# Another order of the blocks inside the steps of a two-direction recurrence

## The reference

```python
def step(S, inp):
    r_t, w_t, kk_t, b_t, v_t, k_t = inp
    sa = jnp.einsum("bhvk,bhk->bhv", S, kk_t)
    S = (S * w_t[:, :, None, :] - sa[..., None] * b_t[:, :, None, :]
         + v_t[..., None] * k_t[:, :, None, :])
    return S, jnp.einsum("bhvk,bhk->bhv", S, r_t)
...
mod = jax.nn.silu(c) @ ada_w[l] + ada_b[l]
sh1, sc1, g1, sh2, sc2, g2 = [m[:, None, :] for m in jnp.split(mod, 6, axis=-1)]
```

## Time and profile before

| | |
|---|---|
| median of 3 runs | 1587.11 us (1568.42 to 1589.66) |
| the profiled execution | 1576.66 us, its span 1575.1 us |
| TensorE busy | 1493.3 us, 95% of the span |
| VectorE, ACT, GpSimd busy | 918.2, 598.1, 271.8 us |
| mean granted TensorE clock | 0.96 of full speed |
| the recurrence's matmuls (L898) | from 243.6 to 528.3 us of the span |

### The profile page before, as it was taken

The page is one execution under the profiler, slowest core; times in us unless marked ns, Lnnn a source line. Parts: engine busy times, 40 slices in busy tenths (PEclk is TensorE's granted clock), DMA queues, the critical chain, the costliest instruction groups (busy, mean ns, idle before and its releaser), DMA issues.

```text
span 1575.1 us, 35522 instructions
## 1 busy us (share of the span) xinstructions
PE 1493.3 (95%) x14858; PEld 1232.4 (78%) x14858; DVE 918.2 (58%) x1499; ACT 598.1 (38%) x1037; POOL 271.8 (17%) x290
## 2 busy tenths in 40 slices
PE   5999989999999998999999998998999999999997
PEld 3788865788889777887877886877878888888885
DVE  4424245676668738888886224767565655555232
ACT  4422345333343534443443223536664322232221
POOL 0000024554443010111111121000021111111110
PEclk9999999778689999999999998999999999999998
DMA  9232201222220222232323222221112232232221
GB/s 370 97 110 79 81 0 56 76 91 84 83 63 4 83 81 80 80 107 80 107 82 108 92 92 81 88 81 55 54 54 82 106 107 85 101 107 92 92 92 72
DMA packets 38987, 139.15 MB, mean 88 GB/s; under 512 B 3152, under 2 KB 3664, under 8 KB 38480
## 3 DMA queue, kind: packets, MB, share of 16 engines
q1 hardware_dynamic: 38720, 135.24, 25.2%
q10 hardware_dynamic: 144, 2.10, 0.3%
HBM read 135.22 MB, written 2.10 MB: 87 GB/s over the span
## 4 chain that ended last, share of the span: by engine, by line
PE 80%; DVE 13%; ACT 3%; issue 3%; DMA 1%; ACTq 0%; DVEq 0%; SPq 0%
PE bank L716 56%; PE bank L898 9%; DVE ffn_sb L3153 5%; PE bank L725 3%; PE bank L662 2%; PE bank L992 1%; DVE w_up L2581 1%; PE bank L1064 1%; PE bank L1004 1%; PE bank L1554 1%; PE bank L929 1%; DMA arena<-w 1%; PE bank L655 1%; ACT w_up L1675 1%; ACT arena L2171 1%
## 5 line engine op out<-in xcount | busy, mean ns | idle before, releaser
L716 PE MATMUL bank<-hf_hi,w_up 128*128 128x512 f32 x1376 | 424.2, 389 | 0.0
L716 PEld LDWEIGHTS bank<-hf_hi,w_up 128*128 128x128 f32 x1376 | 258.4, 188 | 53.2
L716 PE MATMUL bank<-hf_lo,w_up 128*128 128x512 f32 x688 | 269.2, 391 | 4.5 <-DVE w_up L2581 4.5
L716 PE MATMUL bank<-act_hi,w_down 128*128 128x512 f32 x704 | 216.9, 389 | 0.0
L898 PEld LDWEIGHTS bank<-arena 64*64 64x64 f32 x4224 | 160.7, 154 | 35.7 <-issue 25.2
L898 PE MATMUL bank<-arena 64*64 64x32 f32 (+1 forms) x4224 | 172.3, 237 | 10.1 <-issue 6.1
L1675 ACT ACTIVATE w_up<-ring 128x1024 fp32r<-128x1024 f32 x87 | 91.9, 1058 | 215.7 <-PE bank L716 215.7
L2581 DVE TENSOR_TENSOR w_up<-ring,w_up 128x1024 fp32r<-128x1024 f32 x87 | 106.9, 1229 | 96.9 <-ACT w_up L1675 96.9
L716 PEld LDWEIGHTS bank<-hf_lo,w_up 128*128 128x128 f32 x688 | 129.2, 188 | 35.9 <-DVE w_up L2581 8.9
L3153 DVE SCALAR_TENSOR_TENSOR ffn_sb<-ffn_sb 128x512 f32<-128x512 f32 x176 | 151.5, 861 | 5.4
L716 PEld LDWEIGHTS bank<-act_hi,w_down 128*128 128x128 f32 x704 | 132.2, 188 | 27.4
(11 more groups left out here) (350 smaller groups left out, 2399.7 us busy)
## 6 DMA issues: line engine op xcount, KB each, us to landing
ring<-w SPq DMA_DIRECT2D x76, 1024.0 KB, 4.9
ring<-w SPq DMA_DIRECT2D x32, 704.0 KB, 4.0
ring<-w SPq DMA_DIRECT2D x64, 256.0 KB, 3.7
arena<-w SPq DMA_DIRECT2D x8, 1024.0 KB, 18.7
x<-xT SPq DMA_DIRECT2D x1, 2048.0 KB, 9.9
x<-xT ACTq DMA_DIRECT2D x1, 2048.0 KB, 8.4
outT<-x SPq DMA_DIRECT2D x4, 512.0 KB, 2.7
arena<-ctxT SPq DMA_DIRECT2D x1, 1024.0 KB, 18.9
```

The source lines that it names most:

```text
L716: ins = mm(out, w[:, a, k, :], of_block(b, k0 + k), start=first and k == 0 and m == 0, stop=last and k == n - 1 and m == 2)
```

## The change

No instruction that computes is added or removed. The written-out lists are put in another order in all three kinds of steps and on all three engines:

- `scores(q, 1)` moves from level 3 up to right behind level 2's `nx`, ahead of `updates`, and `scores(q, 0)` behind level 2's `dx` (token steps). In the context steps they move to levels 5 and 6.
- `turned(m, 0)` and `turned(m, 1)` move from levels 3 and 4 to level 5, `ada_part(n, 0)` and `(n, 1)` from level 4 and 5 to ahead of and into level 6, `results(n, 1)` ahead of level 4's `dx`.
- `ada_select(n)`, until now in level 6, moves in the token steps to level 3 of the next step, and so does `mod_out`. Two wait counts are changed to fit: `scores(q, 1)` of a token step no longer waits for the sums of the step just before it.
- On VectorE `scores_out`, `first_level`, `running_sums` and `second_result` follow; on ACT `tok_out`, `first_result`, `state_padded`, `update_in` and `ada_row_out`.

The diff, cut to the waits and the token steps (the lists for n = -1 and for the context steps are changed in the same manner):

```diff
@@ -984,7 +984,8 @@
                 done("tok", d, before)
                 done("y_out", d, q - 2 - NCC)
                 if q > 0:
-                    pe.wait_ge(s[("ada_row", "mod")[d]], 8 + min(before, 8))
+                    rows = before - d if q > NCC else before
+                    pe.wait_ge(s[("ada_row", "mod")[d]], 8 + min(rows, 8))
                 n, keys = 2 * L if isx else L, keys_at(d, q)
                 for j in range(NJ):
                     at = slice(2 * L * j, 2 * L * j + n)
@@ -1144,7 +1145,7 @@
                 if n >= 7:
                     return
                 pe.wait_ge(s["ada_row"], 8 + n + 2)
-                done("nk", 1, 2 * n + 4 if n < NCC - 2 else 2 * n + 6)
+                done("nk", 1, 2 * n + 4 if n < NCC - 2 else 2 * n + 8)
                 done("y_out", 1, n - NCC + 1)
                 for m in range(4):
...
             for n in range(NCC - 2, NC - 1):
                 m, q = n + 1, n + 2
                 nx(m, 0, 2)
+                nx(m, 1, 2)
+                scores(q, 1)
                 updates(n, 0)
-                nx(m, 1, 2)
+                dx(m, 1, 2)
+                dx(m, 0, 2)
                 scores(q, 0)
-                dx(m, 0, 2)
-                dx(m, 1, 2)
+                updates(n, 1)
+                nx(m, 1, 3)
+                nx(m, 0, 3)
                 state_terms(n, 0)
                 if n == NC - 2:
                     gate_products(0, 1)
-                updates(n, 1)
-                nx(m, 1, 3)
-                nx(m, 0, 3)
-                scores(q, 1)
-                dx(m, 1, 3)
-                turned(m, 0)
-                dx(m, 0, 3)
                 state_terms(n, 1)
                 if n == NC - 2:
                     gate_products(1, 2)
+                if n > NCC - 2:
+                    ada_select(n - 1)
+                dx(m, 1, 3)
+                dx(m, 0, 3)
                 results(n, 0)
                 nx(m, 0, 4)
-                turned(m, 1)
                 nx(m, 1, 4)
+                results(n, 1)
                 dx(m, 0, 4)
-                results(n, 1)
-                ada_part(n, 0)
                 dx(m, 1, 4)
                 nx(m, 0, 5)
-                ada_part(n, 1)
+                turned(m, 0)
                 nx(m, 1, 5)
                 dx(m, 0, 5)
+                turned(m, 1)
                 dx(m, 1, 5)
+                ada_part(n, 0)
                 nx(m, 0, 6)
-                ada_select(n)
                 nx(m, 1, 6)
+                ada_part(n, 1)
                 dx(m, 0, 6)
                 dx(m, 1, 6)
...
@@ -2008,15 +2010,15 @@
                     for j in range(4):
                         act_f(ycv[0][:, j, :], y_conv[:, j, :], ACT.Copy).then_inc(s["h_hi"], 1)
                 decay_exps(q + 1)
+                update_in(m, 1)
+                first_result(n, 0)
+                first_result(n, 1)
+                tok_out(m, 0)
+                state_padded(m, 0)
                 tok_out(m, 1)
-                first_result(n, 0)
-                update_in(m, 1)
+                state_padded(m, 1)
                 update_in(m, 0)
-                tok_out(m, 0)
                 ada_row_out(n)
-                state_padded(m, 1)
-                first_result(n, 1)
-                state_padded(m, 0)
             split_first("W_OUT")
             for d in range(2):
                 update_out(NC - 1, d)
...
             for n in range(NCC - 2, NC - 1):
                 m, q = n + 1, n + 2
-                w_out(m, 0, 2)
-                running_sums(q + 1, 1)
                 running_sums(q + 1, 0)
                 w_out(m, 1, 2)
-                scores_out(q, 0)
+                w_out(m, 0, 2)
+                scores_out(q, 1)
                 x_out(m, 1, 2)
                 x_out(m, 0, 2)
                 x_turned(m, 0, 2)
+                scores_out(q, 0)
                 x_turned(m, 1, 2)
                 w_out(m, 1, 3)
                 w_out(m, 0, 3)
                 state_out(n, 0)
-                scores_out(q, 1)
+                if n > NCC - 2:
+                    mod_out(n - 1)
+                state_out(n, 1)
                 x_out(m, 0, 3)
                 x_out(m, 1, 3)
-                state_out(n, 1)
+                running_sums(q + 1, 1)
                 x_turned(m, 0, 3)
                 if n == NC - 2:
                     conv_low(0)
                 w_out(m, 0, 4)
-                first_level(q, 1)
+                w_out(m, 1, 4)
+                second_result(n, 0)
                 x_turned(m, 1, 3)
                 if n == NC - 2:
                     conv_low(1)
-                w_out(m, 1, 4)
                 x_out(m, 0, 4)
-                first_level(q, 0)
                 x_turned(m, 0, 4)
                 if n == NC - 2:
                     conv_low(2)
-                second_result(n, 0)
                 x_out(m, 1, 4)
-                w_out(m, 0, 5)
                 x_turned(m, 1, 4)
                 if n == NC - 2:
                     conv_low(3)
+                w_out(m, 0, 5)
+                first_level(q, 1)
                 w_out(m, 1, 5)
+                first_level(q, 0)
                 x_out(m, 0, 5)
                 x_turned(m, 0, 5)
                 x_out(m, 1, 5)
@@ -2985,11 +2989,10 @@
                 x_turned(m, 1, 5)
                 w_out(m, 1, 6)
                 first_turned(q, 0)
+                first_turned(q, 1)
                 y_last(m, 0)
-                first_turned(q, 1)
+                second_result(n, 1)
                 y_last(m, 1)
-                second_result(n, 1)
-                mod_out(n)
```

126 lines of the change are left out of this document (63 added, 63 removed).

## The result

The changed kernel takes 1586.73 us in the median of 20 runs (1578.53 to 1605.32), the kernel before 1587.36 us in the median of 20 (1568.42 to 1596.22). Ratio 1.0073, interval 1.0038 to 1.0108: slower by 0.7%, where 1566 us were forecast. That ratio counts for each kernel only runs within 1.5% of its own fastest; as times here spread evenly over 2 to 3% with the clock, I set the mean of all runs beside it: 1588.1 against 1586.2 us in these two times 20 runs, +2.0 +- 2.6 us, and spans of 1586.5 us (the same 20) against 1583.2 (121 other runs of before, whose spans I have), +3.3 +- 2.0 us. So that the forecast gain did not come is certain; that the whole is slower rests on the ratio and on the split that follows.

What follows compares the result with a forecast made beforehand. TensorE's own work was taken as the bound, lengthened by half clock and standstills. Terms -12.0 - 0.2 + 1.5 + 1.3 + 1.2 + 1.2 - 1.0 - 4.0 + 1.0 = -11.0 us from 1576.66: 1566, range 1544 to 1590.

Steps and rivals of the forecast that it cites:

- The clock: Steps with modulation: thin stretches at step ends go, gain 12.0 us; step from 321.5 gains 1.0; context steps gain 4.0.
- So a thin stretch, not an idle one, costs the clock: Levels 5 and 6: TensorE busy with small products loses the clock, 3.2 us at 0.51 behind; dense work restores it.
- The losses at full clock: Outside the clock: standstills gain 0.2; instruction packets lose 1.5, keys 1.3, VectorE's tail 1.2 and 1.2, the beginning 1.0 us.
- `y_last`: VectorE's step end: comes late behind one more transpose; loss 1.2 us in three steps, 1.2 in four with modulation.
- The first step: At the very beginning, one modulation half and one transpose no longer cover VectorE's first transposes: loss 1.0 us (0 to 1.6).
- Keys: Steps without modulation: scores of direction 1 wait 0.65 us for GpSimd's keys; two steps lose 1.3 us (0 to 3).
- Modulation: Sums cost 0.43 us wherever they stand, so zero; halves ahead of and inside level 6 were to end thin stretches.
- Standstills: Next step's beginning, as weight bursts hold up instruction packets: four at 1.9 us, 7.8 against 8.0, gain 0.2 us.
- Rival C: Slower: standstills behind both scores of a step, low clock lasts; standstills 14.6 instead of 8.0, 1599 us, chance 0.12.
- Rival B: Nothing to be measured: clock falls at standstills as often as at the thin level; 1582 or 1574 us, chance 0.23.
- What would show it: Profile after: full clock in levels 4 to 6, modulation steps 21 to 24 us, standstills near scores, full DMA early.
- the mark of being wrong: Recurrence: summed half-clock time staying near what it was, standstills exceeding 3 us, or scores waiting for keys in all token steps.

Runs made afterwards that it cites:

- e11: Changed kernel with VectorE's two first_level blocks of the token steps put back from level 5 to levels 3 and 4; 1593.6 us, ratio 1.0008.
- e9: Kernel before with unread products added in the first step's two waits, five and three; 1569.4 us, ratio 0.9847.
- e18: Kernel before with paced pieces of weights spread over later levels and small unread products in the first step's two waits; 1556.6 us, ratio 0.9876.
- e4: Kernel before with the two context steps alone in the new order; 1587.8 us, ratio 1.0002.
- e12: e11 with y_last of direction 0 and the running sum also put back as in the kernel before; 1595.4 us, ratio 1.0053.
- e16: e9 with only the token steps' modulation moved: halves to level 6, sums and mod_out to level 3 of the next step; 1579.2 us, ratio 1.003.
- e14: Changed kernel with unread products added in the first step's two waits, five and five; 1588.8 us, ratio 1.0101.
- e5: Kernel before with each paced modulation piece cut to a sixteenth, 16 KB instead of 256 KB; 1575.4 us, ratio 0.998.
- e6: Changed kernel with each paced modulation piece cut to a sixteenth, 16 KB instead of 256 KB; 1570.2 us, ratio 1.0045.

## Why the prediction was wrong

- **The clock: the step that failed.** Forecast -12.0 and -1.0 in steps 3 to 7, -4.0 in the context steps, and no term at all for the last four: together -17.0. Measured -2.9 +- 2, by the time at half of all runs. The profiles say where it went, at 0.42 us per us at half. Steps 3 to 7 gave back 18 +- 6 us at half, about 7.6 us of the 13.0. The context steps gave back nothing. Steps 8 to 11 took 11 to 13 us more at half, about 5 us: TensorE stops there for `x_out`, which `first_level` delays without cover, for a fetch or, in e11, for the keys, and the clock falls behind the stops.
- **"So a thin stretch, not an idle one, costs the clock"** is half right: both do. I counted the falls in the traces' own record of the clock, from step 3 on. In the nine profiles with the old order there are 38. Ahead of 17 of them TensorE and its loads had been idle for less than 0.4 us of the last 4, and each of the 17 lies within 2.7 us of a step's end. In the eleven with the new order or the modulation moved there are 53, and only 3 of them are of that kind. So the thin ends did cost the clock, and the new order did away with those falls. The others come behind stops or shorter waits, and the new order has more idle time. In the kernel before, the fall at 394.9 us comes ahead of the standstill beside it, which begins at 396.0:

```profile
390.80:394.90 4.10, 4.10 (x150) 3.92 (x147) 3.26 (x12) 3.98 (x12) 3.71 (x6) 1.00 0.88 295
394.90:408.50 13.60, 12.26 (x215) 11.97 (x212) 7.54 (x16) 3.94 (x13) 4.73 (x6) 0.50 0.14 49
```

  The Trainium skill ("TensorE: Matmul & The Clock Gate", Part 1) ties the low clock to idleness. The fill of e9 and e18 and the windows over the changed kernel's stops agree with it. These 17 falls and e4's first step, at half clock while busy for 45.73 of 47.20 us, do not.
- **The baseline.** The 53.3 us at half that I read the earlier trace rows were one draw: the time at half of before scatters by 23 us from run to run. Steps 3 to 7 were 11 to 13 us slow in that profile and the first step 20 us fast. I put the sum against that execution, 8 us below the mean, and called the spread chance, but took its parts for properties of the order. The 4.4 us at half in the step from 451.8 and the fall at 490 stood in the rows, yet the last four steps got no term.
- **The losses at full clock**: forecast +6.0 (-0.2 + 1.5 + 1.3 + 2.4 + 1.0), measured +6.2 +- 0.6. The sum is right by luck, for the terms are not. `y_last`: 2.4 forecast, 0 measured (e12). The first step: +1.0 forecast, -1.2 +- 0.7. Keys: 1.3 forecast, 2.3 in e11, and hidden in the changed kernel behind two waits of 1.0 us that I had not priced, `first_level` ahead of `x_out` without cover. Modulation: I wrote "Zero" for the sums, and took the halves' moves for a gain; e16 has +6.7 for the two together.
- **Standstills**: places right. Nine of 0.55 us and more in the changed recurrence, 11.5 us together, against seven and 10.4 in before; from step 3 on 10.3 us against the 8.0 that I read. Rival C had 14.6 instead of 8.0 in the modulation steps and their clock lost behind them. Its mechanism, a stop and then half clock, is the one that came in the last steps, but its price of 22 us was too high and its place wrong: most is lost where few bursts run.
- **Rival B** (1582, or 1574; no gain from the clock) comes nearest in the number. Its reason, that the falls only move to the standstills, holds in part: they went from the ends of steps 3 to 7, and others came behind the stops of steps 8 to 11.
- **What would show it**: most marks came true and the time did not. In the profile after, three of the five steps with modulation last 21 to 24 us (the others 20.8 and 25.0), their levels 5 and 6 run at full clock, and in four of them the DMA row is at 0.9 over the first 3.5 us. The wait of scores for GpSimd was there only once another had been taken away. But the mark of being wrong, time at half in the recurrence that stays near what it is, came true as well: 100 us in the profile after, 87 in that of before.
- **Slips in the working** that change nothing: the clock is below 9 tenths from slice 8 on, not 9; the lowest rate in the burst is 219 GB/s, not 240; four steps at 1.9 us are 7.6, not 7.8.

Still open: what makes up e16's 6.7 us beyond the four waits in its profile, together 4.8 us (TensorE is idle for 3.4 us more than e9's in steps 3 to 7 and 2.9 us more in steps 8 to 11), and why e14's steps 3 to 7 take 122.6 us where the changed kernel's took 113.8; one profile each can't tell it from chance.

## What to carry to other kernels

Where the clock moves between two levels, one profile is one draw: fit span against time at half over all runs before a difference between steps is put down to an order, and give every kind of step a term of its own (here the last four, at which the prediction put no clock, differ by some 10 us between the two orders in all profiles but one). Independent blocks between dependent ones are cover; before one is moved, ask at each place that it leaves what VectorE or GpSimd still has to deliver there. A wait that TensorE can't avoid is cheaper filled with unread products than left idle, and one fill of 3.9 us gave more than the whole reordering was to bring.

## What the runs showed of the hardware

- A stop of TensorE of only 1.0 us was followed by 6.9 us at half clock, 3 us more of work time by the slope of 0.42.
- The clock also falls with no stop: in e5 after 4.20 of 4.20 us busy with small products, then 13.6 us at half.
- The first step runs its 27 us of work in 45 to 51 us if it begins at half clock, and the clock does not come back in it although TensorE counts as busy for 45.73 of 47.20 us (e4).
- VectorE's predicated copies take longer beside GpSimd: in e16 the pair takes 1.32 and 1.62 us while GpSimd runs from 327.45 to 332.17, and 0.89 us where GpSimd pauses:

```profile
381.94 0.89 DVE L2807 COPY_PREDICATED arena<-k_,arena 64x128 f32<-64x128 uint32 x2
```

  The median copy is 444 ns before and 552 ns after, where copies of level 5 stand beside GpSimd's keys (the rows from 493.78 us on above). The Trainium skill ("SBUF — State Buffer", "SBUF: two separate sides") names a port pair that the two engines share as a lock, by which the loser waits for the whole instruction. That they disturb each other the rows agree with; a copy was stretched by 0.2 to 0.4 us.
- Standstills need no burst: with pieces of 16 KB the new order still has five of 0.6 to 1.0 us from step 3 on (e6), the old one one of 0.7 (e5).
